# Full blocks of the second direction moved to other banks and to an earlier place in TensorE's order

## What is computed

```python
def step(s, inp):
    r_t, w_t, k_t, v_t, a_t, b_t = inp
    sa = jnp.einsum('bhvk,bhk->bhv', s, a_t)
    s = s * w_t[:, :, None, :] + sa[..., None] * b_t[:, :, None, :] + v_t[..., None] * k_t[:, :, None, :]
    return s, jnp.einsum('bhvk,bhk->bhv', s, r_t)

s_last, ys = lax.scan(step, s0, xs, reverse=reverse)
```

## Time and profile before

| what | value |
|---|---|
| median of three runs | 2497.02 us |
| the profiled execution's own time | 2493.49 us |
| its span on the core | 2491.6 us |
| TensorE busy | 97% of the span |
| VectorE, ScalarE, GpSimd busy | 51%, 31%, 24% |
| granted TensorE clock, mean | 0.993 |
| the 16 pairs | from 93.9 us to about 1020 us |
| one pair, steady | 57.55 us |

### The profile page before, as it was taken

The page is one execution under the profiler, slowest core; times in us unless marked ns, Lnnn a source line. Parts: engine busy times, 40 slices in busy tenths (PEclk is TensorE's granted clock), DMA queues, the critical chain, the costliest instruction groups (busy, mean ns, idle before and its releaser), DMA issues.

```text
span 2491.6 us, 63941 instructions
## 1 busy us (share of the span) xinstructions
PE 2427.3 (97%) x27968; PEld 1768.6 (71%) x27968; DVE 1277.6 (51%) x2611; ACT 780.4 (31%) x1570; POOL 595.3 (24%) x590
## 2 busy tenths in 40 slices
PE   6999999999999999999999999999999999999998
PEld 1566667666666666668888888856558888775787
DVE  4766666666666665454554243825624434533412
ACT  3445444455545443231220211023400023102301
POOL 2443443334344443100001034400054500000000
PEclk9999999999999998999999999999999999999999
DMA  7111111111111113644336732220144444331353
GB/s 301 50 39 39 47 39 43 43 48 39 39 39 39 44 43 127 226 144 152 135 128 234 252 119 85 85 76 30 51 145 163 136 158 144 127 116 58 108 154 98
DMA packets 80139, 258.19 MB, mean 104 GB/s; under 512 B 11639, under 2 KB 16984, under 8 KB 79096
## 3 DMA queue, kind: packets, MB, share of 16 engines
q1 hardware_dynamic: 75304, 242.94, 29.3%
q0 software_dynamic: 1360, 5.89, 0.7%
q10 hardware_dynamic: 3200, 5.27, 0.6%
HBM read 253.02 MB, written 1.05 MB: 102 GB/s over the span
## 4 chain that ended last, share of the span: by engine, by line
PE 56%; DVE 1%; DMA 1%; ACT 0%; issue 0%; SPq 0%; DVEq 0%; ACTq 0%
PE ps L2012 9%; PE ps L1937 7%; PE ps L2281 7%; PE ps L2067 6%; PE ps L2084 6%; PE ps L2332 5%; PE ps L2135 4%; PE ps L2351 2%; PE ps L2180 2%; PE ps L1861 1%; PE ps L2200 1%; PE ps L2165 1%; PE ps L2220 1%; PE ps L2159 1%; PE ps L2045 1%; DMA ring<-in_w_mods 1%
## 5 line engine op out<-in xcount | busy, mean ns | idle before, releaser
L2012 PE MATMUL ps<-h,ring 128*128 128x256 f32 x1024 | 225.6, 379 | 0.0
L2012 PEld LDWEIGHTS ps<-h,ring 128*128 128x128 f32 x1024 | 193.9, 190 | 34.9 <-issue 9.9
L2067 PE MATMUL ps<-h,ring 128*128 128x256 f32 (+1 forms) x768 | 180.4, 397 | 0.0
L2067 PEld LDWEIGHTS ps<-h,ring 128*128 128x128 f32 x768 | 145.9, 190 | 33.1 <-issue 14.8
L1053 ACT ACTIVATE general<-general 64x512 f32<-64x512 f32 x160 | 101.8, 636 | 161.0 <-DVE general L1252 158.4
L583 PE MATMUL ps<-general,ring 128*128 128x512 f32 x256 | 134.9, 623 | 0.8 <-issue 0.8
L599 PE MATMUL ps<-general,ring 128*128 128x512 f32 x256 | 134.1, 629 | 0.6 <-issue 0.6
L2332 PE MATMUL ps<-h,ring 128*128 128x256 f32 (+1 forms) x480 | 129.1, 422 | 0.0
L774 PEld LDWEIGHTS ps<-general 64*64 64x64 f32 (+1 forms) x5120 | 77.8, 130 | 70.8 <-issue 47.1
L2332 PEld LDWEIGHTS ps<-h,ring 128*128 128x128 f32 x480 | 90.8, 190 | 32.2 <-issue 22.4
L2135 PE MATMUL ps<-ring,h 128*128 128x512 f32 x256 | 110.2, 592 | 0.0
(11 more groups left out here) (442 smaller groups left out, 4859.3 us busy)
## 6 DMA issues: line engine op xcount, KB each, us to landing
ring<-in_w_mods SPq DMA_DIRECT2D x88, 512.0 KB, 4.6
ring<-in_w_feature SPq DMA_DIRECT2D x74, 512.0 KB, 3.2
ring<-in_w_rkvg SPq DMA_DIRECT2D x64, 512.0 KB, 3.7
ring<-in_w_in SPq DMA_DIRECT2D x48, 512.0 KB, 3.2
ring<-in_w_merge SPq DMA_DIRECT2D x48, 512.0 KB, 3.7
ring<-in_w_out SPq DMA_DIRECT2D x32, 512.0 KB, 6.6
ring<-in_w_token SPq DMA_DIRECT2D x24, 512.0 KB, 3.8
ring<-in_w_merge SPq DMA_DIRECT2D x48, 256.0 KB, 3.0
```

Of the source, the lines that this page charges most:

```text
L2012: mm = pe.matmul(ps[:, n % 4, 0:NX], weights(key, k), R.h[:, k, 0:NX], start=(k == 0), stop=(k == KD - 1))
L2067: mm = pe.matmul(ps[:, feature_bank(l, j), 0:width], weights(("feature", l, j), k), R.h[:, k, cols], start=(k == 0), stop=(k == KD - 1))
```

## The change

The second direction's full blocks go to banks 2 and 3, where its own masks no longer have to wait for the first direction's; they are issued right behind the first direction's, ahead of `low(i + 1, 1)`, and wait for `cm_out[0]`, that is, until VectorE has read direction 0's first blocks out of banks 2 and 3. `FILL_MASKS`, the fill that stood behind the second full blocks, is dropped, and the fill behind `below(LAST)` grows from 500 to 1000 columns.

```diff
 FILL_TOKENS = 500
-FILL_MASKS = 500
-FILL_BELOW = (0, 1000, 1000, 1000, 1000, 500)
+FILL_BELOW = (0, 1000, 1000, 1000, 1000, 1000)
...
     def full_blocks(i, z):
         if z:
-            pe.wait_ge(xm_out[0], 2 * (i + 1))
+            pe.wait_ge(cm_out[0], i + 1)
...
-                mm = pe.matmul(ps[:, 4 + h, cx * P:(cx + 1) * P], ...)
+                mm = pe.matmul(ps[:, 4 - 2 * z + h, cx * P:(cx + 1) * P], ...)
...
         first_blocks(i, 1)
         full_blocks(i, 0)
+        full_blocks(i, 1)
         if i + 1 < KE:
             low(i + 1, 1)
         fill(part, FILL_TOKENS)
-        full_blocks(i, 1)
-        fill(part, FILL_MASKS)
...
     def mask_tokens(i, z):
-            src = ps[:, 4 + h, :].rearrange("p (j n) -> p j n", n=2 * P)
+            src = ps[:, 4 - 2 * z + h, :].rearrange("p (j n) -> p j n", n=2 * P)
```

More of the change, by code:

```diff
@@ L751, in full_blocks @@
             for h in range(2):
-                mm = pe.matmul(ps[:, 4 + h, cx * P:(cx + 1) * P], W.bk[rows(h), z, cx, :], W.ar[rows(h), z, cx, :], start=True, stop=True)
+                mm = pe.matmul(ps[:, 4 - 2 * z + h, cx * P:(cx + 1) * P], W.bk[rows(h), z, cx, :], W.ar[rows(h), z, cx, :], start=True, stop=True)
         mm.then_inc(Z("xa_done")[z], 1)
```

## The result

| | median | runs |
|---|---|---|
| before | 2496.37 us | 2490.93 to 2497.84, 12 runs |
| changed | 2502.90 us | 2497.70 to 2506.82, 12 runs |

The ratio is 1.003, with a 95% interval of 1.0021 to 1.0038: 5 to 9 us slower. I had forecast 2512 us, 15 slower. The time lies in my range; the size is off by a factor of more than two.

A forecast was written before the change was run, and what follows sets the result against it. TensorE, busy 97% of the span, was taken to bound the kernel. 14 pairs x 1.05 = 14.7, pair 0 +0.65, pair 15 -1.3, bonus weights +1.0: +15.0 us, median 2512 us; range 2498 to 2519.

The forecast's parts named there:

- What bounds the kernel, and which wait goes: TensorE's own work bounds a pair; `below` of level 1's 0.50 us wait for VectorE's masks goes, nearly to the point.
- The context masks: Second full blocks' new wait for direction 0's context masks costs nothing: masks end at 502.07, blocks start at 503.78.
- What is late next: `low` of direction 1 starts 1.00 to 1.02 us later, moving ScalarE's slackless 5.34 us chain, which `grow` waits for.
- The rival in which the chain does not hold `grow`: Only the wait goes: ScalarE's chain does not hold `grow`, some 8 us gained, 2489 us; chance 0.09.
- The start of `grow`: First `grow` of pair 7 starts at 511.35, the same as before, after ScalarE's move ends at 511.21.
- the term of 1.05 us for the extra piece: One key piece instead of two done before `grow`; the piece left over costs TensorE +1.05 us a pair.
- My price for a pair, 1.12: Steady pair's forecast loss: +1.05 us for the extra piece and 0.07 us for the moved bonus weights.
- Bonus weights: Moved behind the third `grow`, they delay VectorE's adding of level 3 and the fourth `below`: 0.07 us a pair, +1.0.
- Pair 0: First pair, without squares: `grow` can start at 105.3 instead of 105.70, a 1.05 piece is missing: +0.65 us.
- Pair 15: Last pair, without a next one: `below` starts at 967.6 instead of 968.93, -1.3 us; taken as a plain shift.
- The clock: Rival: new gaps of 0.5 and 0.9 us in each pair lower TensorE's clock, 22 us more, 2534; chance 0.04.
- The table load: In ScalarE's chain, taken as 1.28 us without drain; the skill page's 1.38 us drain would cost about 20 us more.

The follow-up runs named there:

- squares late: Changed kernel with ScalarE's squares of the pair before moved behind the first move of the inverse: pair 57.71 us, median 2500.07 us.
- low first: Changed kernel with `low` of direction 1 put ahead of the second full blocks again: pair 57.13 us, median 2493.02 us.
- Old fills: Changed kernel with the filler pieces where they stood before (FILL_MASKS of 500 back, last FILL_BELOW 500): pair 57.41 us, median 2496.73 us.
- one piece less: Changed kernel without one of the eight key pieces of each next pair (k = 6): pair 57.24 us, median 2500.05 us.
- values together: Kernel before with the value piece between the last `below` and `seen_values` moved behind `seen_values`: pair 57.53 us, median 2497.87 us.
- the same in the fastest kernel: Changed kernel with `low` ahead of the second full blocks and the earlier fills, plus the value piece moved behind `seen_values`: pair 56.60 us, median 2487.23 us.
- banks alone: Kernel before with direction 1's full blocks in banks 2 and 3, waiting for cm_out[0], at their old place: pair 57.55 us, median 2498.55 us.

## Why the prediction was right, and where it was wrong

*What bounds the kernel, and which wait goes.* Right, but for 0.1 us. TensorE gets to `below` at 448.30 + 1.02 = 449.32, 0.11 before it starts at 449.43, 0.15 behind the end of VectorE's masks at 446.81 + 2.47 = 449.28; so the masks still hold it a little. The context masks hold nothing.

*What is late next.* Right, and shown by more than the trace: ScalarE's sigmoid of direction 1 waits 2.62 us for `low` instead of 1.73, and the chain behind it ends as `grow` starts. Making the chain shorter by an instruction (squares late) or starting it earlier (low first) moves `grow` and the pair by about as much. The rival in which the chain does not hold `grow` is out.

*The start of `grow`.* 0.19 us earlier than I had it. 0.13 of it is the pair of full blocks, which takes 1.89 together (445.45 to 447.34), so that `low` is 0.89 later and not 1.02. 0.07 is the chain, 5.27 long instead of 5.34: before, the move was held for that long by something else, probably VectorE's transposes, so it was not quite without slack. The release, 0.15 instead of 0.14, takes 0.01 back.

*"TensorE has the same work left plus a piece of 1.05 us ... nothing gives this back. Net: ... +1.05 us a pair."* This is the step that failed: the term of 1.05 us for the extra piece, which measured 0.65. The same work was left in another grouping. Behind the first `grow`, key and value pieces stood in 11 runs before and stand in 9 now, though there is one piece more. A piece is 1.05 between two steps on 64-row tiles, 0.95 with one whole-array neighbour, and 0.86 behind another piece (1.91 for two, have the lone one); the value piece right behind the two small matmuls of the bonus weights is an exception, with 1.03. Summed over the timelines of pair 7 before and pair 6 now, six key pieces took 5.92 us and seven take 6.69, 0.77 more; turning the reads and the `below` behind it became 0.17 shorter, the eight value pieces 0.09 (with the wait below in them); the bonus weights and turned outputs 0.15 longer. That is 0.66, against the 0.65 measured. "Old fills" against the changed kernel has 0.60 for the moved pieces as a whole, "one piece less" 0.86 for the appended one. My price for a pair, 1.12, missed the 0.46 by 0.66: 0.47 of it lies behind `grow` (1.05 and 0.07 forecast, 0.65 measured for both), 0.19 ahead of it.

*Bonus weights.* Right in kind. VectorE copies them as soon as they are there, adds level 3, and the fourth `below` starts 1.15 behind a value piece that takes 1.05 (467.79 to 468.94): 0.10, forecast 0.07. It stands inside the 0.65 (and the 0.66 above).

```profile
467.79 1.10 PE L598 MATMUL ps<-general,ring 128*128 128x512 f32 x2
468.94 1.14 PE L773 MATMUL ps<-general 64*64 64x32 f32 x64
```

*Pair 0.* 56.88 and 56.99 in the two traces, 56.83 before: +0.05 to +0.16, forecast +0.65, and again the piece is what was mis-sized: `grow` came 0.49 us earlier (I had 0.4), and the rest of the pair took 0.54 more in the first trace, where I had 1.05.

*Pair 15.* `below` starts 6.26 us behind the pair's start instead of 7.62, the 1.3 earlier that I had. It is not there at the end: the second half of the next level's `below` was held 2.44 us by a stop called issue (before: 1.69), and then come the next layer's weights. The clock, which I had left open, fell here as it did before: its mean from the pair's start to the next layer is 0.85 and 0.87 in the two traces, 0.87 in that of before. From trace to trace this stretch varies by several microseconds, so I call it neither gained nor lost.

*The sum again*, with measured terms: 14 x 0.46 = 6.4, pair 0 some 0.1: 6.5, and the medians differ by 6.5. That they agree to the tenth is partly luck, since the last pair and the stops vary by several microseconds from trace to trace. My 15.0 had 14 x 1.12 + 0.65 - 1.3.

*The clock.* The profile lists the wait of 0.74 us in 15 pairs, that of 0.33 less than 3 us ahead of it in 13, and the mean of the granted clock over the 15 pairs is 1.00, as before. The Trainium skill (TensorE: Matmul & The Clock Gate, "A second HAM failure mode: psum-queue depth-cycling") has a kernel whose frequent micro-idles made the clock oscillate; gaps of this size and number did not do so here.

*The table load.* In the changed kernel it is in the chain that holds TensorE, so its price matters: 449.70 to 450.99, with no drain behind it. Where the Trainium skill (ScalarE: Activation LUTs, "What ACT_TABLE_LOAD costs") has 1.38 us more, the trace again does not. My estimate from that page, 20 us more, was also worked out wrongly: a longer chain would have held `grow` in the kernel before too, and what the change adds would then be the 1.02 us by which the chain moves, some 15 us more.

## What to carry to other kernels

When a step is moved ahead to remove a wait, look at what it now stands in front of: here `low`, a step of 0.96 us whose consumer had a chain of 5.3 us with next to no slack, hidden until then. Putting the two the other way round took the same idea from 0.3% slower to 0.15% faster, and with the filler pieces back in their old places to 0.55% faster. And a piece of work has no price of its own when the engine changes its tile form around it: count the runs of like steps before and after, not only the pieces.

## What the runs showed of the hardware

For fp32 pieces of 512 columns (two PE instructions each), each change between 64-row tiles and the whole array went with about 0.1 us more on TensorE: 1.05, 0.95 and 0.86 us for a piece with two, one and no such changes around it, in every trace. The exception is the piece behind the bonus weights (1.03). What the engine does in that time no run shows. `below` in tiles of 32 columns took 0.83 us with `seen_values` (64 columns) right behind it, and 0.69 with a whole-array step behind it. And the stops called issue: pairs 1 to 14 lasted longer than 14 steady pairs by 4.9 us in the trace of before, 5.6 and 5.2 in those of the changed kernel, but by 7.1, 6.5 and 9.4 in the three kernels that had taken a piece out from between small matmuls (values together, the same in the fastest kernel, one piece less). With one trace each, and 6.4 in low first and 6.3 in banks alone, which had not, this is a hint and not shown.
